# Three changes of order around weight units: a norm's context half between the query units, a merge rounded unit by unit, and a last chunk kept back for two units

## The reference

```python
# first block, layer i
x  = ffn_step(x, ...);  xc = ffn_step(xc, ...)         # modulate(rms(t)) -> swiglu -> gated add
o_l, o_c = mixer(h_lat=modulate(rms(x), sh2, sc2), h_ctx=modulate(rms(xc), ch2, cc2), ctx_out=ctx_out)
x  = ffn_step(x + g2 * o_l, ...)
# mixer of layer 1, window_gqa: queries of the latents alone (ctx_out is False), keys and values of both
# second block, layer l
proj = rms_norm(x, g_mix[l]) @ w_in[l]
merged = gates[0]*y_a + gates[1]*y_b + gates[2]*y_c + gates[3]*y_d    # y_d = stick_breaking(...) @ w_od
x = x + merged @ w_merge[l]
h2 = rms_norm(x, g_ffn[l])
x = x + (silu(causal_dwconv(h2 @ w_ffn_gate)) * (h2 @ w_ffn_up)) @ w_ffn_down[l]
```

## Time and profile before

| | us |
|---|---|
| median of 3 runs | 3076.77 (3072.92 to 3082.53) |
| the profiled execution, its own time | 3075.38 |
| its span | 3073.7 |
| TensorE busy | 2861.1 (93%) |
| DVE / ACT / POOL busy | 2010.0 / 1176.9 / 523.2 |
| granted TensorE clock, mean of the span | 0.969 |

### The profile page before, as it was taken

The page is one execution under the profiler, slowest core; times in us unless marked ns, Lnnn a source line. Parts: engine busy times, 40 slices in busy tenths (PEclk is TensorE's granted clock), DMA queues, the critical chain, the costliest instruction groups (busy, mean ns, idle before and its releaser), DMA issues.

```text
span 3073.7 us, 43779 instructions
## 1 busy us (share of the span) xinstructions
PE 2861.1 (93%) x18162; PEld 2552.9 (83%) x18162; DVE 2010.0 (65%) x2974; ACT 1176.9 (38%) x1580; POOL 523.2 (17%) x400
## 2 busy tenths in 40 slices
PE   5999999879999999999789999888989998989999
PEld 3888887759888888888747999887989997989999
DVE  3767754476768676465476656985566779756665
ACT  4212254465222251223445334444444443444433
POOL 0200100010101011010000112991000049700000
PEclk8999999999999999999889999999999998999999
DMA  7556532104556454453202666452556663425555
GB/s 242 181 166 185 164 99 83 56 1 122 167 185 192 130 157 137 142 166 113 70 13 67 183 177 177 121 156 89 161 155 171 172 174 108 144 90 178 157 165 145
DMA packets 593174, 427.39 MB, mean 139 GB/s; under 512 B 16848, under 2 KB 571088, under 8 KB 592720
## 3 DMA queue, kind: packets, MB, share of 16 engines
q1 hardware_dynamic: 592976, 424.59, 46.5%
HBM read 423.50 MB, written 1.05 MB: 138 GB/s over the span
## 4 chain that ended last, share of the span: by engine, by line
PE 66%; POOL 12%; DVE 10%; ACT 7%; DMA 3%; issue 3%; SPq 0%; POOLq 0%; ACTq 0%; DVEq 0%
PE ps L716 19%; PE ps L717 18%; PE ps L718 18%; POOL cb_product L2354 6%; DVE w_lo L1612 5%; ACT w_hi L1156 4%; POOL cb_sum L2360 3%; DVE tap_t L2303 1%; PE pm L1014 1%; PE ps L994 1%; DMA raw<-in_w_in 1%; PE ps L1002 1%; POOL cc_product L2354 1%; PE pm L894 1%; PE ps L917 1%
## 5 line engine op out<-in xcount | busy, mean ns | idle before, releaser
L716 PE MATMUL ps<-h_hi,w_hi 128*128 128x256 f32 (+1 forms) x3744 | 1197.5, 320 | 73.4 <-DVE h_lo L1736 23.5
L717 PE MATMUL ps<-h_lo,w_hi 128*128 128x256 f32 (+1 forms) x3744 | 1187.9, 317 | 0.0
L718 PE MATMUL ps<-h_hi,w_lo 128*128 128x256 f32 (+1 forms) x3744 | 1187.3, 317 | 0.0
L1612 DVE TENSOR_TENSOR w_lo<-raw,w_hi 128x2048 fp32r<-128x2048 f32 (+2 forms) x376 | 809.8, 2154 | 357.2 <-ACT w_hi L1156 354.5
L716 PEld LDWEIGHTS ps<-h_hi,w_hi 128*128 128x128 f32 x3744 | 726.1, 194 | 126.7 <-issue 61.3
L1156 ACT CAST w_hi<-raw 128x2048 fp32r<-128x2048 f32 (+2 forms) x376 | 631.1, 1678 | 489.7 <-PE ps L718 306.6
L717 PEld LDWEIGHTS ps<-h_lo,w_hi 128*128 128x128 f32 x3744 | 726.0, 194 | 43.8 <-issue 0.5
L718 PEld LDWEIGHTS ps<-h_hi,w_lo 128*128 128x128 f32 x3744 | 725.4, 194 | 43.3
L2327 POOL TENSOR_TENSOR act_lo<-sil,act_hi 128x512 fp32r<-128x512 f32 (+1 forms) x132 | 160.1, 1213 | 1955.8 <-DVE act_hi L1850 1390.4
L716 PE MATMUL ps<-act_hi,w_hi 128*128 128x256 f32 (+1 forms) x1122 | 368.9, 329 | 8.2 <-POOL act_lo L2327 8.2
L717 PE MATMUL ps<-act_lo,w_hi 128*128 128x256 f32 (+1 forms) x1122 | 367.7, 328 | 0.0
(11 more groups left out here) (276 smaller groups left out, 2997.9 us busy)
## 6 DMA issues: line engine op xcount, KB each, us to landing
chunk_w<-in_ada_t SPq DMA_DIRECT2D x128, 512.0 KB, 3.4
raw<-in_w_in SPq DMA_DIRECT2D x62, 1024.0 KB, 5.4
raw<-in_ffn_pre_wi SPq DMA_DIRECT2D x88, 512.0 KB, 5.3
raw<-in_ffn_post_wi SPq DMA_DIRECT2D x88, 512.0 KB, 5.3
raw<-in_ffn_pre_wo SPq DMA_DIRECT2D x32, 704.0 KB, 4.6
raw<-in_ffn_post_wo SPq DMA_DIRECT2D x32, 704.0 KB, 4.7
raw<-in_w_ffn_gate SPq DMA_DIRECT2D x44, 512.0 KB, 4.0
raw<-in_w_ffn_up SPq DMA_DIRECT2D x44, 512.0 KB, 5.3
```

The source lines that it names most:

```text
L716: pe.matmul(o, hi, x_hi[:, k, tok], start=k == 0, stop=False)
L717: pe.matmul(o, hi, x_lo[:, k, tok], start=False, stop=False)
L718: return pe.matmul(o, weights(w_lo[u.low], u, k, m * P, P), x_hi[:, k, tok], start=False, stop=k == u.run.kc - 1)
L1612: nc.vector.tensor_tensor(w_lo[u.low][:, 0:n], whole[:, 0:n], w_hi[u.slot][:, 0:n].bitcast(F32), ALU.subtract).then_inc(lo_ready, 1)
```

## The change

Three parts of the program are reordered; nothing is computed otherwise, and SP's list of loads is the same.

1. **Context half.** A norm over both halves whose first reader takes latents alone (`gq`, the only such run) is marked `deferred`. TensorE computes unit 0 chunk by chunk, closes it, and then unit 1, with `square_sums` of the context half behind its second chunk. On ACT and DVE the context half moves into `heads`, three chunks behind the split of each of units 2, 3 and so on.
2. **Merge.** ACT rounds the two chunks of `od` unit j right behind the split that stands at j; DVE subtracts those of unit j-1 behind the addition of unit j. DVE's split of the merge run's second unit moves behind the last remainder.
3. **Down-projection.** With latents alone, TensorE takes chunks 0 to 9 of unit 0, then chunks 0 to 9 of unit 1, then waits for chunk 10 and takes it for both.

```diff
     def head_units(run, N, dim, dest, ch0, rot, cos, sin, gain, name=None):
+        shared = stages[-1] if stages[-1].kind == "norm" else None
...
+        if shared is not None and N < shared.N:
+            shared.deferred = u
...
         m = Stage("merge", ready=("merged", br.b["merged"])).takes(m_hi=KC, m_lo=KC)
+        br.next = m
...
             def opening(s, x):
...
+                if norm.deferred is not None:
+                    open_unit(u)
+                    part(u, x, PARTS[0], (name, count)).then_inc(unit_done, 1)
+                    open_unit(v)
+                    part(v, x, PARTS[0], None, (1, norm.st, 1)).then_inc(unit_done, 1)
+                    return
                 open_unit(u)
                 open_unit(v)
...
-                if norm.N == BOTH:
-                    square_sums(norm.st, 1)
...
             def dense_run(s):
...
+                if s.x == "act" and s.N == SEQ:
+                    shared_last(s, x, ready)
+                    start = 2
...
+            def shared_last(s, x, ready):
+
+                two, last = (Unit(s.run, 0), Unit(s.run, 1)), s.run.kc - 1
+                for u in two:
+                    open_unit(u)
+                    for k in range(last):
+                        if u.j == 0:
+                            pe.wait_ge(S[ready[0]], ready[1] + k + 1)
+                        products(u, x, PARTS[0], k, 0)
+                pe.wait_ge(S[ready[0]], ready[1] + last + 1)
+                for u in two:
+                    products(u, x, PARTS[0], last, 0).then_inc(unit_done, 1)
...
@@ ScalarE, heads
+                    deferred = s.opens is not None and s.opens.deferred is s
+                    if deferred and j == 0:
+                        deviations(s.opens.st, 1)
                     if j:
                         deviation(s, j - 1)
                     elif s.tail:
                         deviation(s.tail, s.tail.run.n - 1)
+                    if deferred:
+                        for c in range(3 * j, min(3 * j + 3, KC)):
+                            rounded(s.opens, 1, c)
@@ ScalarE, merge and branch
-            def merge(s):
-
-                for c in range(KC):
-                    act.wait_ge(S["merged"], s.ready[1] + c // 2 + 1)
+            def merged_hi(s, j):
+
+                for c in (2 * j, 2 * j + 1):
+                    act.wait_ge(S["merged"], s.ready[1] + j + 1)
                     nc.scalar.copy(h_hi[:, c, 0:SEQ], merged[:, c, :]).then_inc(S["m_hi"], 1)
+
+            def branch_splits(s):
+                for j in range(s.run.n):
+                    split_ahead(Unit(s.run, j))
+                    if s.next is not None:
+                        merged_hi(s.next, j)
@@ VectorE, proj
-                dve.wait_ge(S["rstd_ready"], st.b["rstd_ready"] + 2)
-                for c in range(KC + 2):
+                if norm.deferred is None:
+                    contexts(norm, 0, KC + 2)
+
+            def contexts(norm, start, end):
+
+                if start == 0:
+                    dve.wait_ge(S["rstd_ready"], norm.st.b["rstd_ready"] + 2)
+                for c in range(start, end):
                     if c < KC:
                         scale(norm, 1, c)
                     if c >= 2:
@@ VectorE, heads
                     split_ahead(Unit(run, i))
+                    if s.opens is not None and s.opens.deferred is s:
+                        contexts(s.opens, min(3 * i, KC + 2), min(3 * i + 3, KC + 2))
@@ VectorE, merge and branch
-            def merge(s):
-                for c in range(KC):
+            def merged_lo(s, j):
+                for c in (2 * j, 2 * j + 1):
                     dve.wait_ge(S["m_hi"], s.b["m_hi"] + c + 1)
...
                 def weigh(u):
-                    split_ahead(u)
+                    if s.next is None or u.j < s.run.n - 1:
+                        split_ahead(u)
                     add_branch(s, u, ps[u.slot][:, :, 0:SEQ])
+                    if s.next is not None and u.j:
+                        merged_lo(s.next, u.j - 1)
...
                 sweep(dve, s.run, weigh)
+                if s.next is not None:
+                    merged_lo(s.next, s.run.n - 1)
+                    split_ahead(Unit(s.run, s.run.n - 1))
```

More of the change, by code:

```diff
@@ L215, in __init__ @@
             self.opens = stages[-1] if stages and stages[-1].kind == "norm" else None
+            self.deferred = None
             self.beside = beside
@@ L1592, in _ @@
                         iw=iw, select=select, glu=glu, cc=cc, plain=plain, stick=stick, layernorm=layernorm, gates=gates,
-                        conv_in=conv_in, proj=proj, branch=splits_only, merge=merge)
+                        conv_in=conv_in, proj=proj, branch=branch_splits)
             act.wait_ge(vec_landed, 16)
@@ L2315, in _ @@
                         select=select, glu=glu, cc=cc, stick=stick, layernorm=layernorm, branch=branch_out, conv_in=conv_in, values=splits_only,
-                        iw=iw, plain=splits_only, gates=splits_only, merge=merge)
+                        iw=iw, plain=splits_only, gates=splits_only)
             nc.vector.memset(cond, 0.0).then_inc(cond_cleared, 1)
```

## The result

| | before | changed |
|---|---|---|
| median of 4 runs | 3076.4 us (3072.92 to 3082.53) | 3035.9 us (3032.75 to 3041.0) |
| profiled execution, its span | 3075.38, 3073.7 us | 3037.48, 3035.8 us |
| mean granted clock | 0.969 | 0.975 |

The ratio is 0.9864, with a 95% interval of 0.9851 to 0.9878: 41.8 us less, 38 to 46. A second measurement of the changed kernel, further down, gives 0.9849 (0.9829 to 0.9870). The prediction was 3037.

A forecast was written before the change was run, and what follows sets the result against it. TensorE, busy 2861.1 of 3073.7 us, was taken as the bound, so only its waits and clock losses could be won. 22 + 8.6 + 9 = 39.6 us off the median 3076.8 gives 3037, range 3026 to 3054.

The forecast's parts named there:

- Part 1, 22 us forecast: Context half at the query units: `gk` read at 1498.1 against 1522.0, less 2 us of deductions; between 15 and 24.
- the 23.9 of the chain: Query units: two units at 7.47 us and `gk` with 12.65 give 1498.1 against 1522.0, before deductions.
- The rival of ACT and DVE as the bound: Query units: DVE work of 8.5 us per unit against 7.47 makes units and loads late; about 3043, chance 0.17.
- Part 2, 8.6 us forecast: The merge in two layers: shorter TensorE wait and earlier end of the run; 8.6 us for both, between 5 and 10.
- a clock that still falls at the merge's waits: Merge: if the clock still drops, unit 0 ends some 1.5 us later, so 3.3 us won instead of 5.0.
- Part 3, 9 us forecast: Six down-projections: 2.85 x 2 + 2.7 + 1.4 less 0.6, put at 9 us, between 3 and 11.
- The idle time of 2.85 us per long site: Two long down-projections: unit 2 starts at 2343.02 and not at 2345.9, 2.85 us won at each.
- 2.7 more: Second long down-projection, in layer 1: 2.7 us more if the shorter wait keeps the clock.
- The 0.6 us for later loads: Down-projections: units 4 and 5 are loaded together and later, a cost of 0.1 us on each of the six.
- The falling clock: Shortened waits in all parts still bring 0.5 clock: part 1 gives 18, part 2 6, part 3 5; about 3049, chance 0.13.
- the slower rival: Low clock lasts through stretches fed chunk by chunk: 99 us lost against 40 won, about 3135; chance 0.03.
- Time that comes back: Attention behind `gk` or the next run's loads end last anyway, so the wait moves: 3070 to 3085, chance 0.05.

The follow-up runs named there:

- `p1_context`: Only part 1, the context half, on the kernel before: 3059.78 us, ratio 0.9933 (0.9920 to 0.9945).
- `defer_only`: `p1_context` with TensorE opening both units before the first chunk, as before; ACT and DVE still spread the context half: ratio 0.9949 (0.9934 to 0.9964).
- `p1_dense`: `p1_context` with six context chunks behind each of the first two query units, not three behind each of four: single run 3060.79 us.
- `p2_merge`: Only part 2, the merge rounded unit by unit, on the kernel before: 3068.86 us, ratio 0.9962 (0.9950 to 0.9975).
- `p3_chunk`: Only part 3, the last chunk kept for two units in all six runs, on the kernel before: 3069.82 us, ratio 0.9964 (0.9951 to 0.9978).
- `before_again`: The kernel before, unchanged, run and profiled once more: 3077.65 us.
- `after_again`: The changed kernel, run and profiled once more: median 3034.17 us (3030.53 to 3040.54).

## Why the prediction was right, point by point

- **Part 1, 22 us forecast, 23.4 measured** in the changed kernel (20.9 in `p1_context`). "Unit 0 ends 0.7 us behind the last chunk, unit 1 waits for its split, the split of unit 2 follows directly" came out within 1 us. I took off 1 us for hand-overs and 1 for a half clock after the 3 us wait. Against the 23.9 of the chain the hand-overs cost 0.5 us; the half clock came in one of the five profiled executions with this opening (`p1_context`), and cost 2.5 us there (45.5 against 43.0).
- **The rival of ACT and DVE as the bound** did not come, with 0.8 us to spare. By my chain unit 0 was read by 1478.8 and its PSUM asked for at 1479.7; it was read by 1478.38 and asked for at 1479.19, in a profile that runs 0.6 us earlier here. `defer_only` and `p1_dense` show that the mechanism exists and what it costs, 2.4 to 2.7 us and, in `p1_dense`, a half clock behind it.
- **Part 2, 8.6 us forecast, 10.2 measured in the merges, 8.2 with what comes back behind them.** The chain was right to 0.4 us (split of unit 0 done 2.0 us behind `od`, I had 2.2; last remainder 7.0, I had 7.4; end 26.8, I had 26.9). I took off 1.4 us for a clock that still falls at the merge's waits: at waits of 2.1 and 0.4 us it did not, in either profile of the changed kernel nor in `p2_merge`. What I had at nothing is the half clock behind the merge, which now lasts longer into TensorE's work and costs 2.0 us more. That the two nearly cancel is luck.
- **Part 3, 9 us forecast; 9.7 between the two profiles, by the lengths of the six runs, and 11.1 (7 to 15) in the times of `p3_chunk`.** The idle time of 2.85 us per long site holds (3.3 less 0.5). The step that was mis-sized is "2.7 more", taken for one site: the clock falls at both in most executions. That one site had kept it was an accident of the execution I read. The 0.6 us for later loads was about right in sum, but not as 0.1 at each run: 0.7 falls on the one run that had no wait to win.
- **The falling clock and the slower rival** fall, on the whole: in both profiles of the changed kernel the stretches fed chunk by chunk run at 1.00. `p1_context` shows that the first of them can come at one place. By the rule of the Trainium skill (TensorE: Matmul & The Clock Gate, A second HAM failure mode), frequent small idles can make the clock swing; with idles of 2.9, 2.1 and 0.4 us in these stretches no profile of the changed kernel shows it.
- **Time that comes back**: 2.0 us do, behind the two merges, by the clock and not by the mechanism that I named. Behind `gk` and the down-projections none recurs in the profiles; the wait for `gk` itself is 4.3 us before and after.
- **The sum.** The steps in the trace come to 23.4 + 10.2 + 9.7 = 43.3 us, the two spans differ by 37.9. Of the 5.4 us between, 2.0 are those behind the merges. The rest are single steps, most of 0.3 to 1.9 us and in both directions, at places that the change doesn't touch, of the kind that `before_again` and `after_again` show between two profiles of one program. So 39.6 forecast and 41.8 measured in the runs agree within the noise of the single terms, and 3037 against 3035.9 is closer than the terms deserve.

## What to carry to other kernels

When two engines feed a third, move work out of the line in front of what the third needs next, and count the whole circle: rounding unit by unit won nothing until the split that stood in it was moved, and spreading work over later units was safe only because it could begin early. Before pricing a clock drop, read the same stretch in a second execution; one profile is one draw. And where a wait goes and its half clock with it, look behind the stretch for where the clock falls next. Then check the smallest margin, here 0.8 us of PSUM, by making it worse on purpose.

## What the chip showed that I had not expected

The same wait of 3.4 us, at the same place of the same program, brings a half clock in one execution and not in another. Over 20 such waits it came 17 times, 15 times for 6.83 us and twice for 3.41. Each time it began before the wait was over, 0.2 to 1.4 us before its end. The 2.9 us wait in part 1 was followed by it in `p1_context`, and in neither profile of the changed kernel. What decides was not found. In the attention behind `gk` the length of the half clock alone is worth 6.3 us between two executions, more than the merge's new order wins in a layer (5.1). And the half clock that the merge lost came back in part behind it, in three profiles of three.
